# Seven saved operands reloaded as high and low parts instead of as one sum that is split again, in a decoder layer on one Trainium2 core

## The chip, the cores and the metric

The kernel runs on one core of a Trainium2 chip. The metric is device time in microseconds. The kernel before takes 2745.06 us, the median of three runs (2744.78 to 2748.09).

## What is computed

A decoder layer over x of 1 x 1024 x 2048 in float32. Cut to what matters here:

```python
ada = c @ w_ada[l] + b_ada[l]
shift, scale, gate = jnp.split(ada, 3, axis=-1)
h = _layer_norm(x) * (1.0 + scale[:, None, :]) + shift[:, None, :]
proj = h @ w_in[l]                     # 2048 -> 9736 columns
(fq, fk, fv, flog, sq, sk, sv, g_fox, g_swa, m_fox, m_swa) = jnp.split(proj, SPLIT_IDX, axis=-1)
o_fox = _forgetting_attention(...)     # 8 heads of 128, causal
o_swa = _sliding_window_attention(...) # 16 query heads of 64, window 128
y_fox = (o_fox * jax.nn.silu(g_fox)) @ w_br_fox[l]
y_swa = (o_swa * jax.nn.silu(g_swa)) @ w_br_swa[l]
merged = jax.nn.sigmoid(m_fox) * y_fox + jax.nn.sigmoid(m_swa) * y_swa
z = DEEPNORM_ALPHA * x + gate[:, None, :] * (merged @ w_out[l])
x = _layer_norm(z) * ln_g[l] + ln_b[l]
```

The part at issue is `h @ w_in`.

## The kernel before

**Products.** TensorE multiplies in float32r. Each float32 operand is split into a high part (a cast to float32r on ScalarE) and a low part (operand minus high part, on VectorE), and a product is three passes: high x high, low x high, high x low. `h @ w_in` is done in groups of 256 output columns, with Strassen's scheme on top: a group is seven products, k = 0 to 6, of combinations of blocks of the weights with combinations of blocks of h. A product is 12 matmuls of 128x128 by 128x512 (4 blocks j, 3 passes), written by `product` (L1791) with the matmul at L1817; `dense` runs a range of them. The seven combinations of h stand in SBUF as b_hi[:, k] and b_lo[:, LO_SLOT[k]], 128 x 2048 elements each, 1 MB.

**Two panels, three phases.** The rows of w_in (the contraction) are done in two panels of 1024, and the results of the second are added in memory (proj_scratch) to those of the first. SBUF holds the seven combinations of one panel only. Groups q = 0 to QKV-1 use the first panel; then b_hi and b_lo are renewed with the second panel's combinations, and all groups run over them, up to Q_FOX-1; then the first panel's combinations come back for the groups from Q_FOX on. QKV = 18 and Q_FOX = 56.

**Saving the combinations.** During groups 1 to 7 SP stores b_hi[:, k] into b_scratch (`save`, L542). From group 9 on GpSimd adds b_lo to it with a store that accumulates (L769), so memory then holds high + low, one float32 array of 1 MB for each k. b_whole counts these.

**Bringing them back.** This is done beside the last unit of the sliding-window attention (`unit_pair(..., last=True)`, L655 to L676). SP walks through k = 0 to 6. It waits for product k of group Q_FOX-1, which is the last reader of these buffers, and from k = 2 on for the load of k-2 (b3_loaded has two semaphores, even and odd). At k = 2 and k = 6 it stores the output tiles 1 and 3 of group Q_FOX-1. Then it issues the load of 1 MB into b_lo. After k = 1 it also issues the first loads of the first forgetting-attention head (`head_rows(0)`, two of `head_q`). After the loop come the stores of tiles 4 and 2, and then `head_in(0)`: the weights of group Q_FOX+1, and the other query tiles, `head_q(0, 2)` first. All of these go through SP's one queue, in this order.

For each k, `again(k)` on ScalarE waits for the load and casts b_lo into b_hi (L1004); `again(k)` on VectorE waits for the cast and subtracts in place (L1596). TensorE waits for b2_lo at the head of product k of group Q_FOX (L1810). again(0) to again(4) are placed by hand between the pieces of the last attention unit, after the work for each product (`passed`); again(5) and again(6) stand at the beginning of head(0).

**The first head.** TensorE's order in `head(0)`: transposes of v, products 0 and 1 of group Q_FOX, scores(0), product 2 and five matmuls of product 3, transposes of weights 0 and scores(1), the rest of 3 and product 4, transposes of weights 1 and scores(2), product 5 and on (FOX_AT, L71). scores(0) needs fq_hi, fk_hi (ScalarE) and their low parts (VectorE). Product 3 needs tile 1 of its group taken out of its bank by ScalarE (`take`, t1_read).

ScalarE waits for two pairs of stores here. Before anything of head(0):

```python
for n in (1, 3):                                  # L1073
    act.wait_ge(stored[n], 16 * GROUPS)           # L1074
```

and, inside head(0), after fk_hi and ahead of the take of tile 1 of group Q_FOX:

```python
for m in (2, 4):                                  # L1121
    act.wait_ge(stored[m], 16 * GROUPS)           # L1122
again(5 + n)                                      # L1123
```

Here stored[n] counts the stores of tile n that SP issues; 16 * GROUPS is reached with the store of group Q_FOX-1.

Of the kernel before, what the change touches and what calls it, by code (L numbers as in the profile page):

```python
# [5 lines left out]
F32 = mybir.dt.float32  # L6
F32R = mybir.dt.float32r
ALU = mybir.AluOpType
ACT = mybir.ActivationFunctionType
AX = mybir.AxisListType  # L10
ds = bass.ds

P = 128
D = 2048
SEQ = 1024
HALF = 512
# [37 lines left out]
LO_SLOT = (1, 0, 6, 4, 5, 3, 2)  # L54
# [70 lines left out]
def build(nc, x, c, w_ada, b_ada, w_in, b_f, attn_sinks, w_br_fox, w_br_swa, w_out, ln_g, ln_b, out):  # L125
# [7 lines left out]

    proj_d = nc.dram_tensor("proj_scratch", (BLOCKS, P, SEQ), F32).ap()
    o_d = nc.dram_tensor("o_scratch", (KD, P, SEQ), F32).ap()
    b_d = nc.dram_tensor("b_scratch", (7, P, 4 * HALF), F32).ap()
    gate_d = nc.dram_tensor("gate_scratch", (1, D), F32).ap()
    cum_d = nc.dram_tensor("cum_scratch", (FOX_HEADS, SEQ), F32).ap()
    q_heads = proj_d[B_SQ:B_SK].rearrange("b (e d) t -> d (b e) t", d=SWA_D)
# [4 lines left out]
    with ctx:  # L144
# [92 lines left out]
        with main:  # L237
# [23 lines left out]
            b_hi = sb("b_hi", [P, 7, 4, HALF], F32R, main)  # L261
# [5 lines left out]
            b_lo = sb("b_lo", [P, 7, 4, HALF], F32R, main)  # L267
# [101 lines left out]
            b2_hi = sem("b2_hi")  # L369
            b2_lo = sem("b2_lo")  # L370
            b_saved = sem("b_saved")
            b_whole = sem("b_whole")
            b3_loaded = [sem("b3_loaded_0"), sem("b3_loaded_1")]
# [117 lines left out]
            def main_sync(sp):  # L491
# [49 lines left out]

                def save(n):  # L542

                    sp.dma_start(b_d[ds(n, 1), :, :].rearrange("a p t -> p (a t)"),
                                 b_hi[:, ds(n, 1), :, :].rearrange("p a j t -> p (a j t)").bitcast(F32)
                                 ).then_inc(b_saved, 16)

# [79 lines left out]
                def unit_pair(g, m, last=False):  # L627
                    u = 2 * m + 8 * g
                    q = 3 * m + (Q_SWA + 12 * g)
                    load_in(q + 1, column(q + (1 - QKV), False), 1)  # L630
                    sp.wait_ge(s_prep, 2 * u + 3)
                    t0 = (2 * m + 1) * P
                    for r in (slice(0, SWA_D), slice(SWA_D, P)):
                        sp.dma_start(sq_raw[r], q_heads[:, ds(8 * g, 8), ds(t0, P)]).then_inc(s_loaded[1], 16)
                        sp.dma_start(sk_raw[r], k_heads[:, ds(2 * g, 2), ds(t0, P)]).then_inc(s_loaded[1], 16)
                    sp.dma_start(sv_raw[:, 1, :], proj_d[ds(g + B_SV, 1), :, ds(t0, P)]
                                 .rearrange("a p t -> p (a t)")).then_inc(s_loaded[1], 16)
                    store_group(q, q - QKV)
                    load_in(q + 2, column(q + (2 - QKV), False), 1)
                    if not isinstance(m, int):  # L640
                        sp.wait_ge(s_prep, 2 * u + 5)
                        t2 = (2 * m + 2) * P
                        for r in (slice(0, SWA_D), slice(SWA_D, P)):
                            sp.dma_start(sq_raw[r], q_heads[:, ds(8 * g, 8), ds(t2, P)]).then_inc(s_loaded[0], 16)
                            sp.dma_start(sk_raw[r], k_heads[:, ds(2 * g, 2), ds(t2, P)]).then_inc(s_loaded[0], 16)
                        sp.dma_start(sv_raw[:, 0, :], proj_d[ds(g + B_SV, 1), :, ds(t2, P)]
                                     .rearrange("a p t -> p (a t)")).then_inc(s_loaded[0], 16)
                    elif not last:
                        attend_in(8, 1, 0)
                    store_group(q + 1, q + (1 - QKV))  # L650
                    if not last:
                        load_in(q + 3, column(q + (3 - QKV), False), 1)
                        store_group(q + 2, q + (2 - QKV))
                    else:
                        load_in(q + 3, column(QKV, False), 0)  # L655
                        sp.wait_ge(b_whole, 16 * 7)
                        for k in range(7):
                            sp.wait_ge(product_done, 7 * (q + 2) + k + 1)
                            if k >= 2:
                                sp.wait_ge(b3_loaded[k % 2], 16 * (k // 2))  # L660
                            if k == 2:
                                store(q + 2, 1, q + (2 - QKV))
                            if k == 6:
                                store(q + 2, 3, q + (2 - QKV))
                            sp.dma_start(b_lo[:, LO_SLOT[k]].rearrange("p j t -> p (j t)").bitcast(F32), b_d[k, :, :]
                                         ).then_inc(b3_loaded[k % 2], 16)
                            if k == 1:
                                sp.sem_inc(f_q, 2)
                                for n in TILES:
                                    sp.wait_ge(added[n], 16 * QKV)  # L670
                                head_rows(0)
                                for i in range(2):
                                    head_q(0, i)
                        store(q + 2, 4, q + (2 - QKV))
                        store(q + 2, 2, q + (2 - QKV))
# [69 lines left out]
            def main_gpsimd(pool):  # L745
# [20 lines left out]
                pool.wait_ge(b_saved, 16 * 7)  # L766
                for k in range(7):
                    pool.wait_ge(n0_ready, 2 * (k + 9))
                    pool.dma_start(b_d[k, :, :], b_lo[:, LO_SLOT[k]].rearrange("p j t -> p (j t)").bitcast(F32),  # L769
                                   accum_op=ALU.add).then_inc(b_whole, 16)  # L770

                def add_tile(q, n, dst):

# [51 lines left out]
            def main_scalar(act):  # L825
# [83 lines left out]
                for p in range(4):  # L909
# [5 lines left out]
                    for K in range(2):  # L915
                        j = 2 * p + K
# [81 lines left out]
                    nc.scalar.activation(sq[:], sq_raw[:], ACT.Copy, scale=SWA_D ** -0.5)  # L998
                    nc.scalar.copy(sk_hi[:, slot], sk_raw[:]).then_inc(s_hi, 1)

                def again(k):

                    act.wait_ge(b3_loaded[k % 2], 16 * (k // 2 + 1))
                    nc.scalar.copy(b_hi[:, k], b_lo[:, LO_SLOT[k]].bitcast(F32)).then_inc(b2_hi, 1)  # L1004

                def unit(g, m, par, last=False):

                    u = 8 * g + 2 * m + par
# [2 lines left out]
                    def passed(lo, hi):  # L1011
                        for n in range(lo, hi):
                            after(q + n // 7, n // 7, n % 7)
                            if last and n >= 16:
                                again(n - 16)

                    act.wait_ge(s_vt, u + 1)
                    nc.scalar.copy(sv[:, par, :, 0, :], tP[:, 0, 0:P].rearrange("p (e d) -> p e d", e=2)
# [58 lines left out]
                def head(h, last=False):  # L1077
                    q = 3 * h + Q_FOX
                    first = isinstance(h, int) and h == 0
# [38 lines left out]
                    for n in range(2):  # L1118
                        if first:
                            if n == 0:  # L1120
                                for m in (2, 4):  # L1121
                                    act.wait_ge(stored[m], 16 * GROUPS)  # L1122
                            again(5 + n)  # L1123
                        after(q, 0, n)
                    for i in range(8):
                        if i < 7:
# [42 lines left out]
            def main_vector(dve):  # L1169
# [343 lines left out]
                def unit(g, m, par, last=False):  # L1513
# [4 lines left out]
                    def passed(lo, hi):  # L1518
                        for n in range(lo, hi):
                            after(q + n // 7, n // 7, n % 7, summed=(n == 10))  # L1520
                            if last and n >= 16:
                                again(n - 16)

                    if par == 1:
                        weight_sums(q + 2, (0, 1))
# [63 lines left out]
                    passed(at[5], at[7])  # L1589
                    half_out(1)  # L1590

                def again(k):

                    dve.wait_ge(b2_hi, 7 + k + 1)
                    low = b_lo[:, LO_SLOT[k]]
                    nc.vector.tensor_tensor(low, low.bitcast(F32), b_hi[:, k].bitcast(F32), ALU.subtract  # L1596
                                            ).then_inc(b2_lo, 1)

                low_parts(0, 0)
                after(Q_SWA - 1, 2, 6)  # L1600
                for g in range(2):
# [18 lines left out]
                def head(h, last=False):  # L1620
                    q = 3 * h + Q_FOX
                    first = isinstance(h, int) and h == 0
# [28 lines left out]
                    dve.wait_ge(f_k_hi, h + 1)  # L1651
                    nc.vector.tensor_tensor(fk_lo[:], fk_raw, fk_hi[:].bitcast(F32), ALU.subtract).then_inc(f_k, 1)
                    for n in range(2):
                        if first:
                            again(5 + n)
                        after(q, 0, n)
                    for i in range(8):
                        dve.wait_ge(f_qk, 8 * h + (i + 2))
# [64 lines left out]
            def main_tensor(pe):  # L1723
# [67 lines left out]
                def product(q, r, k, lo=0, hi=12):  # L1791

                    for n in range(lo, hi):
                        j, part = n // 3, n % 3
                        if n == 0:
                            pe.wait_ge(in_lo, 7 * q + ORDER[k])
                            if k < 3:
                                if not (isinstance(q, int) and q == 0):
                                    if k == 0:
                                        pe.wait_ge(t4_read, q)  # L1800
                                    else:
                                        pe.wait_ge((n0_ready, n1_ready)[k - 1], 2 * q)
                            elif k == 4:
                                pe.wait_ge(n0_ready, 2 * q + 1)
                            else:
                                pe.wait_ge({3: t1_read, 5: t2_read, 6: t3_read}[k], q + 1)
                            if isinstance(q, int) and q == QKV:
                                pe.wait_ge(b2_lo, RENEW.index(k) + 1)
                            if isinstance(q, int) and q == Q_FOX:
                                pe.wait_ge(b2_lo, 7 + k + 1)  # L1810
                            if isinstance(q, int) and q == 0 and k >= 4:
                                pe.wait_ge(b1_lo, LATE_LO[k][1])
                        if isinstance(q, int) and q == 0 and k < 4 and part == 0:
# [700 lines left out]
```

## Time and profile before

| | |
|---|---|
| median of three runs | 2745.06 us |
| profiled execution, its own time | 2749.23 us |
| span of that execution | 2747.6 us |
| mean granted clock of TensorE | 0.988 of full |
| TensorE busy | 2652.3 us |
| VectorE busy | 1813.3 us |
| ScalarE busy | 1136.9 us |
| DMA, mean over the span | 152 GB/s |

Times in the rows are microseconds from the start of the span, of one profiled execution. PE is TensorE, PEld its weight loads, DVE VectorE, ACT ScalarE, POOL GpSimd, SP the queue from which most DMAs go out. L1817 is a line of the kernel. "b_hi<-b_lo" is output from input. A number in square brackets in a timeline is the idle time ahead of the instruction, with what ended it. Matmuls overlap, so one of 0.39 us is followed by the next after less than that.

### The profile page before, as it was taken

To read this page: it belongs to the slowest core of one execution; us is meant where nothing else is said; L and a number is where in the kernel's file an instruction comes from. 1 tells how busy PE (TensorE), PEld (TensorE's weight loads), DVE (VectorE), ACT (ScalarE), POOL (GpSimd) and SP (SyncE) were. 2 spreads that over 40 slices of the span, in tenths; PEclk is the share of its full clock that TensorE was granted. 3 is DMA by queue.
4 is the path that set the end of the run, shared out by engine and by line. 5 is a ranking of instruction groups with operands and counts; after the bars stand their busy time and mean duration, and the time that the engine had idled before them with its cause. 6 is when DMAs were issued, how large, how long until landed. Compare 5 with 4: busy or idle time off the path is not lost.

```text
span 2747.6 us, 39194 instructions
## 1 busy us (share of the span) xinstructions
PE 2652.3 (97%) x12177; PEld 2165.3 (79%) x12177; DVE 1813.3 (66%) x2967; ACT 1136.9 (41%) x2086; POOL 230.4 (8%) x273
## 2 busy tenths in 40 slices
PE   6999999999999999999989999999989999999995
PEld 3578887787877888888878888888868888888884
DVE  7756667686667888888876666666674456544345
ACT  6423335333335555555554444444453332344211
POOL 0000000112120000000001111111100001024000
PEclk9999999999999999999999999999999999999998
DMA  9556773576754444433545545544575455556443
GB/s 315 169 201 224 208 209 108 137 180 144 179 122 113 120 120 120 121 120 120 186 135 127 124 106 122 129 107 110 112 214 162 159 169 177 159 165 200 155 134 111
DMA packets 328893, 418.49 MB, mean 152 GB/s; under 512 B 20392, under 2 KB 231400, under 8 KB 325104
## 3 DMA queue, kind: packets, MB, share of 16 engines
q1 hardware_dynamic: 286144, 343.04, 39.8%
q0 software_dynamic: 29616, 66.12, 13.0%
q10 hardware_dynamic: 13056, 8.39, 1.1%
q8 instruction: 37, 0.61, 0.1%
q14 instruction: 40, 0.33, 0.0%
HBM read 297.90 MB, written 119.59 MB: 152 GB/s over the span
## 4 chain that ended last, share of the span: by engine, by line
PE 87%; DVE 6%; issue 2%; DMA 2%; ACT 2%; SPq 0%; ACTq 0%; DVEq 0%; POOL 0%
PE pA L1817 18%; PE pC L1817 17%; PE pD L1817 17%; PE zP L2485 13%; PE yP L2429 12%; PE tP L1725 2%; PE sP L1966 2%; PE oP L1989 1%; PE sP L1785 1%; DMA b_lo<-b_scratch 1%; PE sP L1751 1%; PE oP L1991 1%; DVE w_lo L1267 1%; PE sP L1908 1%; PE sP L1906 1%
## 5 line engine op out<-in xcount | busy, mean ns | idle before, releaser
L1267 DVE TENSOR_TENSOR w_lo<-w_sum,w_hi 128x512 fp32r<-128x512 f32 x336 | 229.7, 688 | 168.9 <-ACT w_hi L851 168.2
L1817 PE MATMUL pC<-b_hi,w_hi 128*128 128x512 f32 x784 | 308.8, 394 | 7.5 <-DVE b_lo L1241 3.9
L1817 PE MATMUL pA<-b_hi,w_hi 128*128 128x512 f32 x784 | 309.2, 394 | 5.7 <-DVE w_lo L1267 2.8
L1817 PE MATMUL pD<-b_hi,w_hi 128*128 128x512 f32 x784 | 308.1, 393 | 3.3 <-ACT ctile L865 3.3
L1817 PE MATMUL pA<-b_lo,w_hi 128*128 128x512 f32 x784 | 308.1, 393 | 0.0
L1817 PE MATMUL pA<-b_hi,w_lo 128*128 128x512 f32 x784 | 307.8, 393 | 0.0
L1817 PE MATMUL pC<-b_hi,w_lo 128*128 128x512 f32 x784 | 307.7, 392 | 0.0
L1817 PE MATMUL pD<-b_lo,w_hi 128*128 128x512 f32 x784 | 306.3, 391 | 0.0
L1817 PE MATMUL pC<-b_lo,w_hi 128*128 128x512 f32 x784 | 306.3, 391 | 0.0
L1817 PE MATMUL pD<-b_hi,w_lo 128*128 128x512 f32 x784 | 306.0, 390 | 0.0
L178 ACT CAST w_hi<-w_raw 128x1024 fp32r<-128x1024 f32 x128 | 134.8, 1054 | 393.5 <-PE zP L2485 211.1
L183 DVE TENSOR_TENSOR w_lo<-w_raw,w_hi 128x1024 fp32r<-128x1024 f32 x128 | 157.6, 1232 | 174.6 <-ACT w_hi L178 173.8
L851 ACT CAST w_hi<-w_sum 128x512 fp32r<-128x512 f32 x336 | 208.6, 621 | 150.7 <-PE pD L1817 40.4
L775 POOL DMA_DIRECT2D proj_scratch<-ctile x168 | 146.2, 936 | 1466.2 <-DVE ctile L1274 1457.7
L851 ACT CAST w_hi<-w_raw 128x512 fp32r<-128x512 f32 x252 | 156.1, 620 | 172.6 <-PE pD L1817 60.7
L2485 PE MATMUL zP<-w_hi,mg_hi 128*128 128x512 f32 x512 | 199.2, 389 | 0.0
L2485 PE MATMUL zP<-w_lo,mg_hi 128*128 128x512 f32 x512 | 199.2, 389 | 0.0
L2485 PE MATMUL zP<-w_hi,mg_lo 128*128 128x512 f32 x512 | 199.2, 389 | 0.0
L2429 PE MATMUL yP<-og_hi,w_hi 128*128 128x512 f32 x480 | 189.4, 394 | 9.9 <-DVE w_lo L183 7.3
L2429 PE MATMUL yP<-og_lo,w_hi 128*128 128x512 f32 x480 | 188.4, 393 | 0.0
L2429 PE MATMUL yP<-og_hi,w_lo 128*128 128x512 f32 x480 | 188.4, 393 | 0.0
L1817 PEld LDWEIGHTS pC<-b_hi,w_hi 128*128 128x128 f32 x784 | 147.4, 188 | 42.0 <-issue 6.7
(265 smaller groups left out, 5008.1 us busy)
## 6 DMA issues: line engine op xcount, KB each, us to landing
w_raw<-in_w_in_dram SPq DMA_DIRECT2D x168, 512.0 KB, 5.8
proj_scratch<-ctile SPq DMA_DIRECT2D x168, 256.0 KB, 2.2
proj_scratch<-ctile POOLq DMA_DIRECT2D x168, 256.0 KB, 6.0
bg_raw<-in_w_ada_dram SPq DMA_DIRECT2D x64, 512.0 KB, 4.3
w_raw<-in_w_out_dram SPq DMA_DIRECT2D x64, 512.0 KB, 3.9
w_raw<-in_w_br_swa_dram SPq DMA_DIRECT2D x32, 512.0 KB, 4.2
w_raw<-in_w_br_fox_dram SPq DMA_DIRECT2D x32, 512.0 KB, 4.0
aux<-proj_scratch SPq DMA_DIRECT2D x64, 256.0 KB, 4.0
```

The source lines that it names most:

```text
L178: nc.scalar.copy(w_hi[:, slot, :], w_raw[:, slot, :]).then_inc(chunk_hi, 1)
L183: nc.vector.tensor_tensor(w_lo[:, slot, :], w_raw[:, slot, :], w_hi[:, slot, :].bitcast(F32), ALU.subtract).then_inc(chunk_lo, 1)
L775: pool.dma_start(tile_of(dst, n), tiles[n], accum_op=ALU.add).then_inc(added[n], 16)
L851: nc.scalar.copy(ring(k, False), factor(k)).then_inc(in_hi, 1)
L1267: nc.vector.tensor_tensor(ring(k, True), factor(k), ring(k, False).bitcast(F32), ALU.subtract).then_inc(in_lo, 1)
L1725: return nc.tensor.transpose(dst, src, ident[:])
L1751: last = nc.tensor.matmul(row_bank(p), c_sb[:, 4 * slot + k:4 * slot + k + 1], ada_slot(slot)[:, k].rearrange("p s n -> p (s n)"), start=( ...
L1785: last = nc.tensor.matmul(sP[0:32 + FOX_HEADS, T, :], flw_cols[:, c0:c0 + 32 + FOX_HEADS], b[:, j, :], start=(panel == 0 and j == 0 and k ...
L1817: last = nc.tensor.matmul(bank(r, k)[:], w[:, j, :], b[:, j, :], start=(k < 4 and n == 0), stop=(n == 11), skip_group_check=True)
L1966: last = nc.tensor.matmul(dst, fq[:], fk[:, c0:c1], start=(part == 0), stop=(part == 2))
L2429: last = nc.tensor.matmul(dst, w[:, slot, k * P:(k + 1) * P], o, start=(k == 0 and part == 0), stop=(k == 7 and part == 2))
L2485: last = nc.tensor.matmul(zP[:, tb, :], m[:, 2 * kk + k2, tb * P:(tb + 1) * P], w[:, kk % 2, k2 * HALF:(k2 + 1) * HALF], start=(kk == 0 an ...
```

## The change

b_scratch gets a second half, so that for each k it holds b_hi and b_lo as two arrays of 1 MB. GpSimd's store of b_lo no longer accumulates; it writes into the second half. When the combinations come back, SP issues two loads for each k, one straight into b_hi[:, k] and one into b_lo; b3_loaded is counted in 32s. Both `again` functions are gone, with their calls. TensorE waits for b3_loaded directly. The order of everything else on every engine and queue is unchanged.

```diff
-    b_d = nc.dram_tensor("b_scratch", (7, P, 4 * HALF), F32).ap()
+    b_d = nc.dram_tensor("b_scratch", (7, 2, P, 4 * HALF), F32).ap()
...
-                    sp.dma_start(b_d[ds(n, 1), :, :].rearrange("a p t -> p (a t)"),
+                    sp.dma_start(b_d[ds(n, 1), 0, :, :].rearrange("a p t -> p (a t)"),
...
                             if k >= 2:
-                                sp.wait_ge(b3_loaded[k % 2], 16 * (k // 2))
+                                sp.wait_ge(b3_loaded[k % 2], 32 * (k // 2))
                             if k == 2:
                                 store(q + 2, 1, q + (2 - QKV))
                             if k == 6:
                                 store(q + 2, 3, q + (2 - QKV))
-                            sp.dma_start(b_lo[:, LO_SLOT[k]].rearrange("p j t -> p (j t)").bitcast(F32), b_d[k, :, :]
-                                         ).then_inc(b3_loaded[k % 2], 16)
+                            for part, b in enumerate((b_hi[:, k], b_lo[:, LO_SLOT[k]])):
+                                sp.dma_start(b.rearrange("p j t -> p (j t)").bitcast(F32), b_d[k, part, :, :]
+                                             ).then_inc(b3_loaded[k % 2], 16)
...
-                    pool.dma_start(b_d[k, :, :], b_lo[:, LO_SLOT[k]].rearrange("p j t -> p (j t)").bitcast(F32),
-                                   accum_op=ALU.add).then_inc(b_whole, 16)
+                    pool.dma_start(b_d[k, 1, :, :], b_lo[:, LO_SLOT[k]].rearrange("p j t -> p (j t)").bitcast(F32)
+                                   ).then_inc(b_whole, 16)
...
-                def again(k):
-
-                    act.wait_ge(b3_loaded[k % 2], 16 * (k // 2 + 1))
-                    nc.scalar.copy(b_hi[:, k], b_lo[:, LO_SLOT[k]].bitcast(F32)).then_inc(b2_hi, 1)
...
-                            if last and n >= 16:
-                                again(n - 16)
...
-                            again(5 + n)
...
-                def again(k):
-
-                    dve.wait_ge(b2_hi, 7 + k + 1)
-                    low = b_lo[:, LO_SLOT[k]]
-                    nc.vector.tensor_tensor(low, low.bitcast(F32), b_hi[:, k].bitcast(F32), ALU.subtract
-                                            ).then_inc(b2_lo, 1)
...
                             if isinstance(q, int) and q == Q_FOX:
-                                pe.wait_ge(b2_lo, 7 + k + 1)
+                                pe.wait_ge(b3_loaded[k % 2], 32 * (k // 2 + 1))
```

## Rows read from the trace of the kernel before

**Rows 1.** The page, section 1: busy time, share of the span, instructions.

```profile
PE 2652.3 (97%) x12177; PEld 2165.3 (79%) x12177; DVE 1813.3 (66%) x2967; ACT 1136.9 (41%) x2086; POOL 230.4 (8%) x273
```

**Rows 2.** Stages: stretch, its length; busy PE, PEld, DVE, ACT, POOL; clock, DMA share, GB/s.

```profile
260.00:400.00 140.00, 140.00 (x619) 115.90 (x618) 87.10 (x125) 46.33 (x79) 6.21 (x7) 1.00 0.79 220
1355.00:1375.00 20.00, 18.91 (x96) 15.62 (x95) 15.60 (x21) 11.92 (x23) 0.00 (x0) 1.00 1.01 373
1365.00:1370.00 5.00, 5.00 (x27) 4.21 (x26) 4.85 (x6) 3.04 (x4) 0.00 (x0) 1.00 1.00 396
1361.00:1375.00 14.00, 12.91 (x61) 10.40 (x61) 11.07 (x14) 10.38 (x21) 0.00 (x0) 1.00 1.02 417
1370.00:1375.00 5.00, 3.91 (x19) 2.93 (x18) 4.43 (x5) 3.39 (x5) 0.00 (x0) 1.00 1.04 432
1375.00:1393.00 18.00, 9.73 (x40) 7.48 (x39) 15.48 (x18) 11.79 (x13) 0.00 (x0) 0.91 0.89 304
1393.00:1400.00 7.00, 6.18 (x21) 4.69 (x21) 6.38 (x10) 3.95 (x8) 0.87 (x1) 0.76 0.01 3
1420.00:1560.00 140.00, 139.62 (x696) 116.99 (x695) 93.16 (x201) 65.32 (x139) 18.25 (x21) 1.00 0.54 124
```

**Rows 3.** Waits of TensorE's matmuls in 1355 to 1420: us in total, times, longest.

```profile
PE oP L1927 <- DVE spT_lo L1567: 4.5, 1, 4.5
PE sP L1966 <- issue: 3.8, 1, 3.8
PE tP L1725 <- DVE fp_w L1673: 1.1, 1, 1.1
PE pD L1817 <- ACT ctile L865: 1.1, 1, 1.1
```

**Rows 4.** The chain that ended last, 1345 to 1410: start, length, what.

```profile
1364.42 10.32 DMA b_lo<-b_scratch
...
1388.22 0.65 ACTq L1056
...
1402.74 2.72 PE pA L1817 x12
```

**Rows 5.** Instructions on b_lo: count, ns min/median/max, first and last start.

```profile
L769 POOL DMA_DIRECT2D b_scratch<-b_lo x7: 851/853/1065, 277.9 to 391.8; - x7
...
L1004 ACT CAST b_hi<-b_lo x7: 1905/1908/1917, 1364.9 to 1393.6; 128x2048 fp32r<-128x2048 f32 x7
L1596 DVE TENSOR_TENSOR b_lo<-b_lo,b_hi x7: 2287/2292/2293, 1366.8 to 1395.5; 128x2048 fp32r<-128x2048 f32 x7
L1443 DVE TENSOR_TENSOR b_lo<-h_raw,b_hi x6: 2284/2286/2289, 439.6 to 466.3; 128x2048 fp32r<-128x2048 f32 x6
```

**Rows 6.** Timeline of TensorE's matmuls: start, length, what, idle time before.

```profile
1369.25 1.03 PE L1725 MATMUL tP<-ident,sp_w 128*128 128x128 f32 x8
...
1393.01 0.30 PE L1966 MATMUL sP<-fk_hi,fq_hi 128*128 128x128 f32 x1 [3.80 <-issue]
...
1393.97 0.63 PE L1817 MATMUL pD<-b_lo,w_hi 128*128 128x512 f32 x1
...
1400.32 0.33 PE L1725 MATMUL tP<-ident,fp_w 128*128 128x128 f32 x1 [1.14 <-DVE fp_w L1673]
...
1406.16 0.39 PE L1817 MATMUL pC<-b_hi,w_hi 128*128 128x512 f32 x1
```

**Rows 7.** DMA issues at 1364.0, 1380.9 and 1376 to 1378: size, us to landing.

```profile
proj_scratch<-ctile SPq DMA_DIRECT2D x1, 256.0 KB, 8.2
...
proj_scratch<-ctile SPq DMA_DIRECT2D x1, 256.0 KB, 2.5
...
b_lo<-b_scratch SPq DMA_DIRECT2D x1, 1024.0 KB, 4.9
```

**Rows 8.** Timeline of ScalarE (fq_hi, the take of tile 1) and VectorE (its join).

```profile
1389.04 0.31 ACT L1084 ACTIVATE fq_hi<-fq_raw 128x128 fp32r<-128x128 f32 x1 [6.10 <-DVE so_st L1572]
...
1393.08 0.60 ACT L865 COPY ctile<-pC 128x512 f32<-128x512 f32 x1
...
1397.72 0.68 DVE L1274 TENSOR_TENSOR ctile<-pA,ctile 128x512 f32<-128x512 f32 x1
```

More of the change, by code:

```diff
@@ L1520, in passed @@
                             after(q + n // 7, n // 7, n % 7, summed=(n == 10))
-                            if last and n >= 16:
-                                again(n - 16)
                     if par == 1:
@@ L1653, in head @@
                     for n in range(2):
-                        if first:
-                            again(5 + n)
                         after(q, 0, n)
```

## The prediction

> **What bounds the kernel now.** I read the page's busy table first: TensorE is busy for 97% of the span [rows 1]. Work that VectorE and ScalarE shed is therefore worth time only where TensorE waits for it. The table of stages then shows where that is: in the whole stretch where the combinations are first written out, 260 to 400 us, TensorE is busy 140.00 of 140, and in 1420 to 1560 us 139.62 of 140. Where they come back, at 1355 to 1400 us, it has holes: 9.73 of 18 us in 1375 to 1393, and DMA there is at 1.01 and 0.89 of its capacity, with 373 and 304 GB/s [rows 2]. TensorE's waits of that stretch are four: 1.1, 4.5, 3.8 and 1.1 us, 10.5 in all [rows 3]. The chain of waits runs through it as a load of a combination, 10.32 us [rows 4], after which casts of about 1.91 us on ScalarE and subtractions of 2.29 us on VectorE follow one another [rows 5]. So the change aims at a real stall; it also doubles the traffic on a resource that is full there.
>
> **The write-out, 260 to 400 us.** Seven accumulating stores of 1 MB become plain stores of the same size from the same queue. TensorE has no hole there to win [rows 2]. The first who waits for b_whole is the cast of renewed combinations at L968, whose first subtraction comes at 439.6 us, 48 us after the last of these stores is issued at 391.8 [rows 5]. I cost it at 0, from both sides: nobody waits for them to be faster, and were they slower, most of those 48 us cover it.
>
> **What is removed.** Seven casts (7 x 1.91 = 13.4 us on ScalarE) and seven subtractions (7 x 2.29 = 16.0 us on VectorE) [rows 5]. They make all four waits. The wait of 4.5 us (for spT_lo) goes: turned_high and turned_low no longer stand behind again(0) to again(2), and the transposes that they read ran at 1369.25 [rows 6]. The wait of 1.1 us for ctile L865 goes likewise. The wait of 3.8 us (before scores(0)) stands behind ScalarE and VectorE, which come out of these pieces late (fq_hi only at 1389.04 [rows 8]). So from 1393.01, 9.4 us of waits earlier, TensorE could be at scores(0) near 1383, with products 0 and 1 of Q_FOX done. What is late next decides.
>
> **What is added: bytes in one FIFO.** Every load and store of this stretch except one stands on SP's queue. That it is served in order is seen in rows 7: a 256 KB store issued at 1364.03, behind two loads of combinations and those for the first head, takes 8.2 us to land, while one that meets an emptier queue at 1380.9 takes 2.5. In 1361 to 1375 us the DMA engines moved 417 GB/s at 1.02 of the engines' time [rows 2]. A further 1024 KB (1.049 MB) thus costs 1.049/417 = 2.51 us for everything behind it, and a pair 5.03 us. The loop over k issues pair k once pair k-2 has landed; a pair stays in the queue for longer than landing takes (a load that meets an almost empty queue lands in 4.9 us, of which 2.5 are its bytes [rows 7]), so the queue doesn't run dry, and I add bytes only.
>
> Anchor: now the load of k = 2 lands at 1364.42 + 10.32 = 1374.74 [rows 4], with the queue full until then. After the change three more parts stand ahead of that point (k = 0, 1, 2): + 3 x 2.51 = 1382.3. ScalarE's store of so_st (256 KB, 0.63 us), which now goes out at 1388.2 [rows 4], will go out near 1377, into this queue's time: 1382.9. Pair 3 lands at 1387.9, pair 4 at 1393.0.
>
> **Who stands behind these bytes.** SP issues the store of tile 3 of group Q_FOX-1 in turn k = 6, after waiting for pair 4 (1393.0). Pair 5 is ahead of it: 1398.0, and its own 0.63 us: it lands at 1398.6. ScalarE waits for exactly this store at L1074, ahead of everything of the first head (fq_hi, fv_hi, fk_hi). Today that wait hides under the casts, the store having been issued at 1380.9 and landed 2.5 us later [rows 7] while ScalarE reached it just ahead of fq_hi at 1389.04. Behind it: fq_hi at 1389.04, the casts of v and k, VectorE's low parts, and scores(0) on TensorE at 1393.01, 3.97 us later [rows 6, 8]. So scores(0) comes at 1398.6 + 3.97 = 1402.6, not 1393.0. TensorE is idle from about 1383 to 1402: waits of 1.1, 4.5 and 3.8 us are replaced by one of about 19.
>
> From scores(0) to the start of product 5 TensorE takes 1406.16 - 1393.01 = 13.15 us now, of which 1.14 are the last of the four waits, behind again(6) [rows 6]; I take 12.0. It includes the granted clock after an idle spell: 0.76 over 1393 to 1400 [rows 2], with matmuls of 0.63 us [rows 6]. Product 5 then starts at 1414.6, against 1406.16: **8.4 us later**.
>
> A second chain gives nearly the same. Tiles 4 and 2 are stored only after pair 6: 1398.6 + 5.03 + 2 x 0.63 = 1404.9. ScalarE waits for both at L1122 before it takes tile 1 of Q_FOX, and product 3 and the first softmax stand behind that: 0.6 us for the take [rows 8], then from the join at 1397.72 to the start of product 5 another 8.4 us: 1413.9. The wait that ends last is the first, by 0.7 us. The third, the load of the query tile for scores(2), comes behind tiles 4 and 2 and one pair of weight loads, about 1404.9 + 3 to 5; with some 3 us of softmax behind it, it ends at or a little before the same point. From product 5 onward all data are there and TensorE is busy, 139.62 of 140 us [rows 2], with no slack to absorb the delay.
>
> **Sum.** scores(0) comes 1402.6 - 1393.0 = 9.6 us later, and the way from there to product 5 is 1.15 us shorter: +8.4. Against the profiled execution (2749.23 us, span 2747.6 plus 1.6 around it) that is 2757.6. That execution lies 4.2 us above the median 2745.06; on the median, 2753.5.
>
> **A rule of the Trainium skill against it.** The 14 us around 1361 to 1375 show 417 GB/s, nearly all of it reads from memory [rows 2]. The Trainium skill, page DMA: Bandwidth & Descriptors, section Where 436 GB/s comes from, says that for transfers between HBM and SBUF the HBM side limits a core to about 358 GB/s; the trace disagrees over 14 us, but the changed kernel asks for this rate for 40. Its page HBM Reference (Specifications) allows a core that streams alone about 425 GB/s, which the trace bears out better. By that rule the 10 MB would cost an estimated 27.9 us instead of 23.9, and the delay would be 12.3.
>
> **The rivals.**
> - Faster: TensorE held by the landing of the pairs alone. This is so if the tile stores don't suffer from the queue (they land about 2.5 us after issue, and ScalarE's waits stay hidden), and the query tile too. Pair 6 lands at 1398.6 + 5.0 = 1403.6, and product 6 starts there. Now it starts no earlier than 1406.16 + 2.72 (a product, rows 4) = 1408.9: -5.3, so 2739.8, or a little less. For it: the 10.5 us are real. Against it: the 8.2 us store of rows 7, and that the store is not even issued before pair 4 is down. It turns slower once the store of tile 3 lands later than about 1390.2 (8.4 us before my 1398.6), and pair 4 alone lands after that. 0.10.
> - No change that can be measured: the queue serves small stores out of turn, or bytes overlap better than 2.51 us a part, and half of the delay goes: +3 to +5, 2748 to 2750. 0.13.
> - Slower still: memory doesn't hold 417 GB/s over the 18 MB of this stretch. At 373 GB/s, the mean of 1355 to 1375 with its tile stores and weight loads [rows 2], the 10 MB counted above (nine parts, a tile store and so_st) cost 26.8 us instead of 23.9: +11.3, so 2756.4. 0.05.
> - The forecast: 0.72.
> That the change doesn't do what it says is no case of its own: the casts and subtractions are out of the program.
>
> **Range.** Rates of 396 to 432 GB/s (two slices of 5 us in rows 2) give +1.3 and -0.8 us on the 10 MB. The last part of the sum at 13.15 instead of 12.0 gives +1.1. After 20 us of idleness TensorE may stay at the lower of its clocks for longer than the 3.6 us seen after the wait of 3.8 (the granted clock of 0.76 over 7 us is 1.7 us lost [rows 2]): up to +1.7. Landings may be 1 us off either way, and the median itself moves by 1 to 3. That gives +5.5 to +12.5; down to +3 for most of the no-change case. Range 2748.0 to 2758.5. About 0.2% (5.5 us) is what a measurement of this kernel can tell from no change: slower 0.73, same 0.17, faster 0.10.
>
> **What would show it.** In the changed trace: loads of 2 x 1024 KB at above 400 GB/s without a hole from 1360 to about 1402; no wait of TensorE for spT_lo; scores(0) near 1402 after some 20 us idle, with ScalarE idle before fq_hi; casts of k and v starting 1 us after the store of tile 3 lands; product 5 of Q_FOX near 1414. Wrong if TensorE has only short holes before each product of Q_FOX (then the pairs bind, and the time falls), or if 260 to 400 us shows a hole.

## The result, and the profile of the changed kernel

The changed kernel takes 2756.22 us (median of 7), the kernel before 2747.79 us (median of 7 in the same comparison): ratio 1.0034, 95% interval 1.0024 to 1.0043. By the medians it is 8.4 us slower, by the ratio 9.3 (6.6 to 11.8). Its profiled execution has a span of 2757.2 us, 9.6 more than the one of before. Of these 9.6, 1.2 are there already when the first load of a combination is issued (1357.06 against 1355.88), which is scatter between executions: these starts lie between 1352.84 and 1357.06 in the profiles of this study. Where two traces are compared below, I count from that issue.

(In the part above, the product should read 2048 to 10760 columns, not 9736: the sizes into which proj is split add up to 10760.)

TensorE's waits from 1355 to 1420 us, which answer to [rows 3]:

```profile
PE sP L1948 <- issue: 20.7, 1, 20.7
```

Four waits of 10.5 us have become one of 20.7, before scores(0) of the first head. The stages (the columns are those of [rows 2]):

```profile
260.00:400.00 140.00, 140.00 (x620) 115.93 (x620) 86.62 (x125) 45.36 (x79) 3.91 (x7) 1.00 0.65 225
...
1360.00:1402.00 42.00, 22.84 (x109) 18.70 (x107) 16.08 (x29) 12.44 (x27) 0.00 (x0) 0.81 1.02 417
1383.00:1403.00 20.00, 0.00 (x0) 0.00 (x0) 2.27 (x4) 2.33 (x4) 0.00 (x0) 0.58 1.01 420
1403.00:1410.00 7.00, 6.45 (x17) 5.31 (x18) 2.61 (x9) 1.91 (x6) 0.86 (x1) 0.50 0.72 238
1420.00:1560.00 140.00, 139.62 (x694) 116.77 (x693) 92.62 (x197) 64.00 (x135) 20.03 (x23) 1.00 0.52 121
```

The read-out is plain: from 1360 to 1402 us DMA is full (1.02 of its time, 417 GB/s) and TensorE works 22.84 of 42 us. From 1383 to 1403 no compute engine does anything to speak of, while DMA moves 420 GB/s. The write-out at 260 to 400 us has no hole of TensorE's, before or after, and the matmuls of the two traces stay the same 0.49 us apart all through it.

From product 5 on the trace is that of before, 10.6 to 10.7 us later (9.4 if the 1.2 are taken off), until near 2040 us. There TensorE waits for VectorE once more, in both kernels, and this wait is 0.9 us shorter in the changed one; the spans end 9.6 apart:

```profile
2041.08 0.77 PE L2429 MATMUL yP<-og_hi,w_hi 128*128 128x512 f32 x1 [6.42 <-DVE w_lo L183]
...
2050.77 0.77 PE L2411 MATMUL yP<-og_hi,w_hi 128*128 128x512 f32 x1 [5.52 <-DVE w_lo L183]
```

In the profiles of this study this wait is 6.0 to 6.5 us in the kernel before and the three experiments built on it, and 5.1 to 5.5 in the changed kernel and those built on it, but for 6.0 in e9_hybrid_345. It doesn't follow the delay (6.5 in e2_two_loads, the slowest of all, 5.2 in the fast e7_hybrid). What sets it stays open.

The chain of waits, followed back from scores(0), names what is waited for (start, length, what):

```profile
1369.43 14.02 DMA b_lo<-b_scratch
...
1383.89 10.04 DMA b_lo<-b_scratch
...
1393.98 5.53 DMA proj_scratch<-ctile
...
1399.59 0.32 ACT fq_hi L1078
```

1369.43 + 14.02 is the landing of pair 2, 1383.89 + 10.04 that of pair 4. Then comes the store of tile 3 and then ScalarE's first instruction of the head. ScalarE's own timeline has the two waits for stores that the prediction named (in brackets the idle time ahead):

```profile
1399.59 0.31 ACT L1078 ACTIVATE fq_hi<-fq_raw 128x128 fp32r<-128x128 f32 x1 [22.47 <-DMA proj_scratch<-ctile]
...
1405.77 0.59 ACT L866 COPY ctile<-pC 128x512 f32<-128x512 f32 x1 [3.83 <-DMA proj_scratch<-ctile]
```

And TensorE's, from scores(0) to the first matmul of product 5:

```profile
1403.55 0.44 PE L1948 MATMUL sP<-fk_hi,fq_hi 128*128 128x128 f32 x1 [20.71 <-issue]
...
1409.66 0.54 PE L1799 MATMUL pC<-b_hi,w_hi 128*128 128x512 f32 x1
...
1416.74 0.39 PE L1799 MATMUL pC<-b_hi,w_hi 128*128 128x512 f32 x1
```

### The profile page after: what moved, and what is told of

Same layout as the page of the kernel before. It is cut to its first block, busy times and chain, and to the rows that moved or that the text cites. A ratio compares the mean times of both kernels' runs of the same rounds, so it can differ in the third digit from the quotient of the medians.

```text
span 2757.2 us, 39187 instructions
## 1 busy us (share of the span) xinstructions
PE 2652.0 (96%) x12177; PEld 2167.8 (79%) x12177; DVE 1797.1 (65%) x2960; ACT 1124.1 (41%) x2079; POOL 228.8 (8%) x273
## 4 chain that ended last, share of the span: by engine, by line
PE 88%; DVE 5%; DMA 3%; issue 2%; ACT 2%; SPq 0%; ACTq 0%; DVEq 0%; POOL 0%
PE pA L1799 18%; PE pC L1799 18%; PE pD L1799 18%; PE zP L2467 12%; PE yP L2411 12%; PE tP L1707 2%; PE sP L1948 2%; DMA b_lo<-b_scratch 1%; PE oP L1971 1%; PE sP L1767 1%; PE sP L1733 1%; PE oP L1973 1%; PE sP L1890 1%; PE sP L1888 1%; PE oP L1912 1%
```

## The experiments

Ratios are against the kernel before, run on the same chip in the same session (medians of before: 2747.13, 2747.65 and 2747.53 us in the three sessions). Two kernels whose intervals overlap are not told apart by the ratio; where their single runs don't overlap, I say so. Where I say that one wait took the place of another, it is the trace that says so.

### The two halves of the change, one at a time

**e1_no_split**: the casts and subtractions out, no bytes added.

```diff
-                                again(n - 16)
...
-                            again(5 + n)
...
-                                pe.wait_ge(b2_lo, 7 + k + 1)
+                                pe.wait_ge(b3_loaded[k % 2], 16 * (k // 2 + 1))
```

> The kernel before without its casts and subtractions: each combination comes back in one load of 1 MB (the sum, into the low buffer), the high buffer keeps the second panel's values, so the products from group Q_FOX on have wrong operands; all loads, stores and waits for them stay. It measures what removing the splits is worth without the added bytes. Theory (the splits cost the three waits, the queue then sets the end): TensorE has products 0 and 1 done by about 1382; the store of tile 3 is issued when load 4 lands (about 1379.7) and lands near 1383.5; scores(0) at 1387.5, product 5 near 1399.5 instead of 1406.2: 6 to 7 us faster than before (about 2741). Rival (the 10.5 us of waits go whole): 10 us faster. Rival (the splits were not the cause of the waits): within 2 us of before.

Measured: 2741.78 us, ratio 0.9981 (0.9972 to 0.999), 5.3 us faster. One wait of TensorE is left in this stretch:

```profile
PE sP L1959 <- issue: 6.8, 1, 6.8
```

The splits did cause the four waits. Of their 10.5 us about half are gained; a wait of 6.8 us is left, for the store of tile 3, which was issued at 1380.03 behind load 5 and took 4.4 us. (The products from group Q_FOX on have wrong operands here, as in e11_plain_write; the instructions and their waits are what counts.) So even with 7 MB the queue is what is late next.

**e2_two_loads**: the bytes added, the casts and subtractions kept.

```diff
-                            sp.dma_start(b_lo[:, LO_SLOT[k]].rearrange("p j t -> p (j t)").bitcast(F32), b_d[k, :, :]
-                                         ).then_inc(b3_loaded[k % 2], 16)
+                            for b in (b_hi[:, k], b_lo[:, LO_SLOT[k]]):
+                                sp.dma_start(b.rearrange("p j t -> p (j t)").bitcast(F32), b_d[k, :, :]
+                                             ).then_inc(b3_loaded[k % 2], 16)
```

> The kernel before with the sum loaded twice, into the high and into the low buffer, then cast and subtracted as before: the added 7 MB alone, with the splits kept. Theory (bytes in SP's queue decide): the splits now hide behind the loads except the last; scores(0) near 1403 and product 5 at 1416 to 1417: 9.5 to 11 us slower than before, and only 1 to 3 us slower than the changed kernel. Rival (the changed kernel is slower through something other than the bytes, such as waiting on the loads directly): within 3 us of before.

Measured: 2763.72 us, ratio 1.0062 (1.0048 to 1.0075), 16.6 us slower: more than I expected. The chain shows what I had missed:

```profile
1393.85 9.75 DMA proj_scratch<-ctile
1403.61 1.91 ACT b_hi L1005
1405.55 2.32 DVE b_lo L1597 x2
```

again(5) stands behind ScalarE's wait for the stores of tiles 4 and 2, as the listing of the kernel shows. I had let it run before that wait. With the queue full, the store lands at 1403.6. Two casts and two subtractions come only after it, and the second subtraction ends at 1410.1. The direction is as forecast: 7.3 MB cost 16.6 us with the splits in place, and 8.4 + 5.3 = 13.7 us without them. At 417 GB/s they are 17.6 us of queue time.

**e11_plain_write**: the write side alone.

```diff
-                    pool.dma_start(b_d[k, :, :], b_lo[:, LO_SLOT[k]].rearrange("p j t -> p (j t)").bitcast(F32),
-                                   accum_op=ALU.add).then_inc(b_whole, 16)
+                    pool.dma_start(b_d[k, :, :], b_lo[:, LO_SLOT[k]].rearrange("p j t -> p (j t)").bitcast(F32)
+                                   ).then_inc(b_whole, 16)
```

> The kernel before with only the write side changed: GpSimd's seven stores of the low parts no longer accumulate (so memory holds only the low parts, and products from group Q_FOX on have wrong operands). Casts, subtractions, waits and bytes of the reload stay. Theory (TensorE has no hole at 260 to 400 us): the time of before within 2 us (its medians here are 2747 to 2748). Rival (the accumulating stores held something up, or the plain ones do): 3 us or more away from it.

Measured: 2747.08 us, ratio 1.0 (0.9991 to 1.0009). The write side is worth nothing that can be told here: the interval is 2.5 us either way.

### Which wait holds the first head

**e3_stores_early** moves the three tile stores ahead of pair 4.

```diff
-                            if k == 6:
-                                store(q + 2, 3, q + (2 - QKV))
+                            if k == 4:
+                                for n in (3, 4, 2):
+                                    store(q + 2, n, q + (2 - QKV))
...
-                        store(q + 2, 4, q + (2 - QKV))
-                        store(q + 2, 2, q + (2 - QKV))
```

> The changed kernel with the stores of tiles 3, 4 and 2 of group Q_FOX-1 issued ahead of pair 4 instead of ahead of and behind pair 6. Same bytes, same queue, other order. Theory (ScalarE's waits for these stores hold the first head): the stores land near 1390 instead of 1399.5 and 1405.5, scores(0) near 1394 to 1395, and then the query tile for scores(2), behind pair 6 and the weights, ends last: product 5 near 1411 to 1413, 3 to 5 us faster than the changed kernel (about 2752). Rival (the landing of the pairs binds TensorE): no difference to the changed kernel within 1 us.

Measured: 2755.1 us, ratio 1.0028 (1.0018 to 1.0039). TensorE's waits:

```profile
PE sP L1947 <- issue: 11.7, 1, 11.7
PE tP L1706 <- DVE fp_w L1654: 5.3, 1, 5.3
```

By the time alone this could be the rival's case (no difference). The trace decides: scores(0) came at 1394.30, 9.0 us sooner than in the changed kernel, counted from the first load, and then ScalarE waited for the query tile of scores(2) until 1410.4:

```profile
1410.39 0.31 ACT L1077 ACTIVATE fq_hi<-fq_raw 128x128 fp32r<-128x128 f32 x1 [8.37 <-DMA fq_raw<-proj_scratch]
```

So the mechanism is as expected, and product 5 at 1413.49, 3.0 us sooner, is near what I expected. The time is not: I expected 3 to 5 us and it is within 1 us or so of the changed kernel. The waits are 3.7 us shorter in sum (17.0 against 20.7), but there are two of them, and after each TensorE's granted clock is at its lower level for a while (mean 0.56 over 1394 to 1401 us and 0.65 over 1411 to 1420 us). The second such stretch is the loss:

```profile
1411.84 0.69 PE L1706 MATMUL tP<-ident,fp_w 128*128 128x128 f32 x2 [5.32 <-DVE fp_w L1654]
...
1413.49 0.63 PE L1798 MATMUL pC<-b_hi,w_hi 128*128 128x512 f32 x1
```

From these transposes to the start of product 6 (1418.57) it takes 6.7 us, against 4.2 in the changed kernel (1415.88 to 1420.11), where the matmuls of product 5 take 0.39 us instead of 0.63. So 2.5 of the 3.7 us go to the clock, and product 6 starts 1.3 us sooner.

**e4_queries_early** also puts query tiles 2 and 3 ahead of the weights of group Q_FOX+1.

```diff
-                        if i == 0:
+                        if i == (3 if first else 0):
                             load_in(q + 1, column(q + (1 - GROUPS), False), 0)
```

> As e3_stores_early, and the query tiles 2 and 3 of the first head are loaded ahead of the weights of group Q_FOX+1. Theory: the query tile lands 3 to 4 us earlier than in e3_stores_early, near 1406, so product 5 starts near 1408 to 1409: 6 to 8 us faster than the changed kernel, 1 to 3 us slower than before. If pair 6 then ends last, the gain over e3_stores_early stays under 2 us. Rival (pairs bind): no difference to the changed kernel.

Measured: 2752.46 us, ratio 1.0023 (1.0013 to 1.0032), 3.8 us below the changed kernel where 6 to 8 were expected. The two intervals overlap, but all eleven runs (2750.71 to 2755.46) lie below all seven of the changed kernel (2755.71 to 2758.89). The second wait fell from 5.3 to 3.1 us; the first stayed at 11.7. From the start of product 5 to that of product 6 it takes 5.2 us, with matmuls of 0.63 us at first, as in e3_stores_early (5.1), against 3.4 in the changed kernel.

**e5_wait_late** moves the wait and leaves the queue alone.

```diff
-                for n in (1, 3):
-                    act.wait_ge(stored[n], 16 * GROUPS)
...
-                                for m in (2, 4):
+                                for m in TILES:
```

> The changed kernel with ScalarE's wait for the stores of tiles 1 and 3 moved from ahead of the first head's fq_hi, fv_hi and fk_hi to the place where it waits for tiles 4 and 2. Nothing else moves. Theory (two chains behind the same queue, the second only 1 us shorter): scores(0) comes at once, near 1383, product 2 too, and TensorE then waits about 20 us for tile 1 to be taken, until the stores of tiles 4 and 2 land near 1405.5; product 5 comes 0 to 2 us earlier than in the changed kernel. Rival (the wait at the head of the first head is the whole cause): 8 us or more faster than the changed kernel, the time of before or better.

Measured: 2754.85 us, ratio 1.0032 (1.0019 to 1.0044). In the trace the idle time has the same length and has moved behind product 2, to the take of tile 1. Product 5 comes 0.6 us later than in the changed kernel, counted from the first load, where 0 to 2 us earlier was expected.

```profile
PE pC L1797 <- ACT ctile L866: 20.6, 1, 20.6
PE pD L1797 <- DMA b_lo<-b_scratch: 0.6, 1, 0.6
```

Both chains of the prediction are thus real. The second alone gives the whole loss here, and in the changed kernel, where TensorE waits for nothing after scores(0), the first does. The rival, that the wait at L1074 is the one cause, falls.

**e8_pool_stores** issues these stores from GpSimd's queue.

```diff
-                                store(q + 2, 3, q + (2 - QKV))
...
-                        store(q + 2, 4, q + (2 - QKV))
-                        store(q + 2, 2, q + (2 - QKV))
...
+                for n in (3, 4, 2):
+                    tile_done(pool, Q_FOX - 1, n)
+                    pool.dma_start(tile_of(2 * (GROUPS - 1), n), tiles[n]).then_inc(added[n], 16)
```

(The waits for them count `added[n]` accordingly.)

> The changed kernel with the stores of tiles 3, 4 and 2 of group Q_FOX-1 issued from GpSimd's queue instead of SP's. Theory (they are late because they stand in line in SP's queue): issued near 1377, they land within 6 us although SP's queue is full, scores(0) comes near 1386 to 1388, and the query tile behind pair 6 and the weights ends last: product 5 within 1.5 us of e3_stores_early, 1 to 3 us faster than the changed kernel. Rival (they are late because the DMA engines are full, whatever the queue): they land after 1395 and the time is that of the changed kernel.

Measured: 2754.61 us, ratio 1.0029 (1.0018 to 1.004), no different from e3_stores_early. Issued at 1370.4, 1373.2 and 1373.7, the stores landed 7.5, 7.0 and 8.4 us later, not within 6, beside a full queue of SP's (the row has the median of the last two):

```profile
proj_scratch<-ctile POOLq DMA_DIRECT2D x2, 256.0 KB, 7.7
```

In the changed kernel the store of tile 3 took 5.5 us in SP's own queue. A queue of its own therefore made it no faster; what helped is that it didn't have to wait for its turn in SP's program, 20 us later. scores(0) came at 1381.93 after a wait of 3.1 us. TensorE then waited 11.3 us for the softmax behind the query tile, the third chain.

### Can the bytes be afforded in a better order?

**e6_queue_reordered** has all seven pairs and moves everything that someone waits for ahead in the queue; ScalarE waits for the stores late, as in e5_wait_late.

```diff
-                            if k == 6:
-                                store(q + 2, 3, q + (2 - QKV))
+                            if k == 3:
+                                for n in (3, 4, 2):
+                                    store(q + 2, n, q + (2 - QKV))
+                            if k == 5:
+                                for i in range(2, 4):
+                                    head_q(0, i)
+                            if k == 6:
+                                load_in(q + 4, column(q + (4 - GROUPS), False), 0)
```

> All seven pairs as in the changed kernel, same bytes, with every waiting instruction's data moved ahead in SP's queue: the stores of tiles 3, 4 and 2 ahead of pair 3, query tiles 2 and 3 ahead of pair 5, the weights of group Q_FOX+1 ahead of pair 6; ScalarE's store waits late as in e5_wait_late. Theory (what costs is who stands behind the bytes, and then the bytes themselves): TensorE is held by each pair in turn (short waits of about 2 us before products 3 to 6), product 6 ends near 1409 to 1410: 2 to 5 us faster than before, so 10 to 13 us faster than the changed kernel. Rival (14 MB at 420 GB/s end last whatever their order, and TensorE's clock falls in the waits): no better than before.

Measured: 2749.7 us, ratio 1.0009 (1.0 to 1.0018): 6.5 us better than the changed kernel, but not faster than before, where 2 to 5 us were expected. With the same 14 MB the order, and ScalarE's waits for the stores moved behind as in e5_wait_late, thus give back most of the 8.4 us. The rival holds. TensorE's waits:

```profile
PE pC L1810 <- DMA b_lo<-b_scratch: 6.1, 2, 4.5
PE oP L1982 <- DVE fpT L1627: 4.4, 1, 4.4
PE pA L1810 <- DMA b_lo<-b_scratch: 1.1, 1, 1.1
```

Pair 3 now holds product 3 for 4.5 us (three stores went ahead of it), and the weights landed at 1404.2, for which ScalarE and VectorE waited 6.9 and 6.8 us in the middle of the head: a fourth consumer that I had not priced. With 14 MB something always stands last in the queue.

**e7_hybrid** is this order with pairs for k = 0, 1, 2, 6 only. k = 3, 4, 5 come back as sums, split in the first head.

```diff
+PAIRS = (0, 1, 2, 6)
...
+                        if first and i == 0:
+                            again(3)
+                            again(4)
...
+                        if first and i == 1:
+                            again(5)
```

> e6_queue_reordered with pairs for k = 0, 1, 2 and 6 and sums, cast and subtracted, for k = 3, 4 and 5, placed in the first head where ScalarE and VectorE are idle: 11 MB instead of 14. Theory: the three splits hide in idle time and pair 6 lands 7.5 us sooner: 3 to 6 us faster than e6_queue_reordered, 6 to 10 us faster than before. Rival (VectorE's three subtractions of 2.3 us come onto the path again): no faster than e6_queue_reordered.

Measured: 2744.42 us, ratio 0.9993 (0.9984 to 1.0002): 5.3 us better than e6_queue_reordered as expected (their single runs hardly overlap: 2743.60 to 2748.34 against 2747.66 to 2752.85), but only 3 below before, where 6 to 10 were expected and which its interval doesn't separate. One long wait is left, for the subtraction of k = 3:

```profile
PE pC L1836 <- DVE b_lo L1630: 7.5, 1, 7.5
```

**e9_hybrid_345** is e7_hybrid with the tile stores behind the load of k = 3, and ScalarE waits for each store only ahead of that tile's own take.

```diff
+                            if k == 3:
+                                for n in (4, 2, 3):
+                                    store(q + 2, n, q + (2 - QKV))
...
+                            if first and n in (2, 3, 4):
+                                act.wait_ge(stored[{2: 4, 3: 2, 4: 3}[n]], 16 * GROUPS)
```

> e7_hybrid (pairs for k = 0, 1, 2, 6, sums for 3, 4, 5) with the stores of tiles 4, 2 and 3 issued behind the load of k = 3 instead of ahead of it, and ScalarE waiting for each tile's store only ahead of its own take. Theory (product 3 waits for the load of k = 3, its cast and subtraction, with 0.8 MB of stores ahead of them in the queue): that load lands about 2 us sooner, product 3 starts 2 us sooner: 1 to 3 us faster than e7_hybrid, 4 to 6 us faster than before. Rival (the wait only moves to product 4 or 5): within 1 us of e7_hybrid.

Measured: 2743.12 us, ratio 0.9984 (0.9975 to 0.9993): faster than the kernel before by 4.4 us, and so than the changed one by 12.8 (8.4 + 4.4). The wait for k = 3 went from 7.5 to 6.0 us. The 1.3 us to e7_hybrid are not told apart, so between 1 to 3 us and the rival's "within 1 us" this run doesn't decide.

**e10_hybrid_456** is the same with pairs for 0 to 3 and sums for 4 to 6.

```diff
-PAIRS = (0, 1, 2, 6)
+PAIRS = (0, 1, 2, 3)
...
-SPLITS = (3, 4, 5)
-AGAIN = {2: (3, 4), -1: (5,)}
+SPLITS = (4, 5, 6)
+AGAIN = {2: (4,), -1: (5,), 4: (6,)}
```

> As e9_hybrid_345 with pairs for k = 0 to 3 and sums for 4, 5 and 6: same bytes. Theory: a pair for k = 3 lands 2.5 us later than a sum but needs no cast and subtraction (4.2 us), so product 3 starts 1 to 2 us sooner than in e9_hybrid_345; products 4 to 6 then depend on splits that follow 2.5 us later: within 2 us of e9_hybrid_345 either way. Rival (splits of late combinations end last): 2 to 5 us slower than e9_hybrid_345.

Measured: 2750.37 us, ratio 1.0013 (1.0004 to 1.0022), 7.3 us slower than e9_hybrid_345 with the same bytes. The rival holds, with more than it said:

```profile
PE pA L1840 <- DVE b_lo L1633: 4.9, 1, 4.9
PE oP L2012 <- DVE fpT L1651: 4.2, 1, 4.2
PE pC L1840 <- DMA b_lo<-b_scratch: 2.7, 1, 2.7
```

Product 3 did start sooner: its wait is 2.7 us instead of 6.0. But product 4 then waits 4.9 us for the split of k = 4, whose load landed at 1389.3, and the split of k = 6 (cast at 1401.0) stands on both engines ahead of the attention's fpT, which TensorE then waits for.

## Why the prediction was right, point by point

The forecast was 8.4 us more, and 8.4 were measured between the medians. The mechanism is right step by step, as the table shows. That the number agrees to the tenth is luck: product 5 came 9.4 us later and not 8.4, one of these was taken back by the shorter wait near 2040 us, and the ratio gives 9.3. The forecast median of 2753.5 was low by 2.7 us because the kernel before, at 2745.06 in three runs, has a median of 2747.79 in seven. The steps, with the prediction's times moved by the 1.2 us of the later start:

| step | predicted | in the trace |
|---|---|---|
| pair 2 has landed | 1384.1 | 1383.44 |
| pair 4 has landed | 1394.2 | 1393.93 |
| the store of tile 3 has landed | 1399.8 | 1399.51 |
| scores(0) | 1403.8 | 1403.55 |
| tiles 4 and 2 have landed (take of tile 1) | 1406.1 | 1405.77 |
| product 5 | 1415.8 | 1416.74 |

- **The write-out costs nothing**: right, shown by e11_plain_write within 2.5 us, and more closely by 140.00 of 140 us and by the unchanged distance of the two traces there.
- **The waits behind the splits go**: right. e1_no_split shows it by itself, and shows too that removing them alone wins only 5.3 us, since the store of tile 3 is late next.
- **The queue is served in order**: right by all landings. One reading behind it was off: the store that took 8.2 us, issued at 1364.03, had one load of a combination ahead of it, not two, since that of k = 0 had landed at 1363.97. Nothing in the sum rests on it.
- **2.51 us for each MB, for everything behind it**: right within 0.7 us over seven landings (those of the table, and pair 3 at 1388.71, pair 5 at 1398.88 and pair 6 at 1404.44; tiles 4 and 2 landed at 1405.08 and 1405.75). The DMA engines stayed at 417 GB/s for 42 us.
- **The Trainium skill's 358 GB/s** (page DMA: Bandwidth & Descriptors, section Where 436 GB/s comes from) doesn't bind here: 417 GB/s over 42 us. Its page HBM Reference (section Specifications (TRN2)), which allows a core streaming alone about 425, agrees with the trace.
- **ScalarE's wait for the store of tile 3 decides, the stores of tiles 4 and 2 nearly so**: right. e5_wait_late takes the first chain away and gets the second at the same price, e3_stores_early and e8_pool_stores make both short and get the third, the query tile.
- **12.0 us from scores(0) to product 5**: wrong by 1.2. It was 13.19. TensorE's granted clock was 0.50 (1.2 of 2.4 GHz) over 1403 to 1410 us, after 20.7 us of idleness; product 2 took 1409.66 - 1404.43 = 5.2 us where before it took 4.4. The prediction had this only in its range (up to +1.7). Product 5 came 0.9 us after its forecast.
- **From product 5 on there is no slack to absorb the delay**: wrong by 1.0, by the wait near 2040 us.
- **The second chain ends 0.7 us before the first**: not shown. In the trace of e5_wait_late, where it is alone, product 5 comes 0.6 us later than in the changed kernel, and the times of the two are not told apart.

Two things the prediction didn't ask came out in the experiments. My sizes for the repairs were too large. In e3_stores_early and e4_queries_early two short waits cost nearly as much as one long one, because TensorE comes out of each at the lower clock (2.5 us of it in e3_stores_early, by its trace). In e6_queue_reordered there was one more consumer behind the same bytes than I had counted, the weights.

## What to carry to other kernels

Before trading arithmetic for bytes, list everything that is issued in the same queue behind the new transfers, small stores and their buffer-reuse waits above all, and follow each to who waits for it; the bytes delay each of them by the same time, and curing one exposes the next (four in a row here). A split, cast or other cheap step that runs on an idle engine can be cheaper than the transfer that replaces it: the best kernel of this study doubles the bytes only where the engines were busy (k = 0, 1, 2 and, last in line, 6) and splits where they were idle. A wait placed early in an engine's program for a resource that is needed late was hidden here until the queue filled; put each directly ahead of the instruction that needs it. (Moving one alone gained nothing, in e5_wait_late; it is part of the best kernel.)

## What the runs showed of the hardware

```profile
q1 hardware_dynamic: 572, 4.16, 94.0%
q10 hardware_dynamic: 527, 0.26, 8.3%
...
o_scratch<-so_st ACTq DMA_DIRECT2D x1, 256.0 KB, 14.9
```

- The granted clock fell to 0.5 in the idle spell of 20.7 us and stayed there through scores(0) and the 5.2 us of product 2, whose matmuls took 0.63 us each. After the wait of 3.8 us in the kernel before, the last four matmuls of product 2 were at 0.39 us again, and the product took 4.4 us. After the wait of 5.3 us in e3_stores_early, product 5 took 5.1 us instead of 3.4 (start to start of product 6).
